# The expert down products with the weight matrix stationary and 160 rows moving, their outputs summed and turned ahead of the scatter

## The reference

```python
probs = jax.nn.softmax((hf @ router).astype(F32), axis=-1)
top_p, top_i = lax.top_k(probs, TOP_K)
top_p = top_p / jnp.sum(top_p, -1, keepdims=True)
gates = jnp.sum(jax.nn.one_hot(top_i, N_EXPERTS, dtype=F32) * top_p[..., None], axis=1)
out = jnp.zeros_like(hf)
for e in range(N_EXPERTS):          # 8 experts
    out = out + gates[:, e:e + 1] * _swiglu(hf, wg[e], wu[e], wd[e])
# _swiglu(h, wg, wu, wd) = (silu(h @ wg) * (h @ wu)) @ wd, 1024 -> 1408 -> 1024
```

## Time and profile before

| | |
|---|---|
| median of 3 runs | 3254.36 us (3253.84 to 3255.85) |
| profiled execution | 3251.81 us, span 3250.0 us |
| TensorE busy (products) | 89% of the span |
| VectorE busy | 49% |
| ScalarE busy | 33% |
| mean granted TensorE clock | 0.938 |

### The profile page before, as it was taken

The page is one execution under the profiler, slowest core; times in us unless marked ns, Lnnn a source line. Parts: engine busy times, 40 slices in busy tenths (PEclk is TensorE's granted clock), DMA queues, the critical chain, the costliest instruction groups (busy, mean ns, idle before and its releaser), DMA issues. The chain is left out here.

```text
span 3250.0 us, 41841 instructions
## 1 busy us (share of the span) xinstructions
PE 2897.2 (89%) x16468; PEld 2532.3 (78%) x16468; DVE 1606.1 (49%) x2087; ACT 1075.4 (33%) x1404; POOL 132.4 (4%) x111
## 2 busy tenths in 40 slices
PE   7999769999799997779999999969999685789997
PEld 5889768878678896679999999958788564668785
DVE  3536744232434466357777777763332437442333
ACT  2334113222232332035555555442222323242221
POOL 0012100000000220010000000000000000000000
PEclk9999989999899998879999999979999896799998
DMA  4210025151322001166767767742341210251421
GB/s 142 92 45 1 1 91 146 40 142 46 97 78 78 16 1 52 40 186 195 203 196 214 202 194 207 202 129 80 96 112 33 91 26 2 66 148 46 136 59 65
DMA packets 441223, 324.88 MB, mean 100 GB/s; under 512 B 22880, under 2 KB 395616, under 8 KB 440960
## 3 DMA queue, kind: packets, MB, share of 16 engines
q1 hardware_dynamic: 439360, 317.06, 34.1%
q0 software_dynamic: 1728, 5.90, 0.6%
HBM read 318.19 MB, written 4.72 MB: 99 GB/s over the span
## 5 line engine op out<-in xcount | busy, mean ns | idle before, releaser
L1467 PE MATMUL psum<-x_split,gate_up_split 128*128 128x512 f32 x1056 | 414.6, 393 | 15.8 <-PEq L1636 7.8
L1468 PE MATMUL psum<-x_split,gate_up_split 128*128 128x512 f32 x1056 | 413.9, 392 | 0.0
L1469 PE MATMUL psum<-x_split,gate_up_split 128*128 128x512 f32 x1056 | 413.5, 392 | 0.0
L2476 PE MATMUL psum<-x_slots_split,gate_up_split 128*128 128x320 f32 x1424 | 378.4, 343 | 4.4 <-DVE x_slots_split L2654 2.5
L1759 PE MATMUL psum<-w_split,x_split 128*128 128x256 f32 (+1 forms) x2400 | 300.0, 287 | 33.1 <-ACT w_split L1773 13.2
L1759 PEld LDWEIGHTS psum<-w_split,x_split 128*128 128x128 f32 x2400 | 295.8, 196 | 38.4 <-ACT w_split L1773 27.1
L2477 PE MATMUL psum<-x_slots_split,gate_up_split 128*128 128x160 f32 x1424 | 314.7, 241 | 0.0
L1759 PE MATMUL psum<-x_split,w_split 128*128 128x512 f32 x1248 | 295.2, 396 | 15.8 <-DVE w_split L1793 6.2
L1570 DVE TENSOR_TENSOR arena<-arena,psum 128x512 f32<-128x512 f32 x66 | 45.4, 688 | 513.9 <-ACT arena L1525 513.9
L1759 PEld LDWEIGHTS psum<-x_split,w_split 128*128 128x128 f32 x1248 | 235.5, 190 | 75.9 <-issue 20.6
L2476 PEld LDWEIGHTS psum<-x_slots_split,gate_up_split 128*128 128x128 f32 x1424 | 261.6, 189 | 10.3 <-issue 7.3
(11 more groups left out here) (423 smaller groups left out, 4485.8 us busy)
## 6 DMA issues: line engine op xcount, KB each, us to landing
arena<-in_moe_w_gate SPq DMA_DIRECT2D x91, 512.0 KB, 4.4
arena<-in_moe_w_up SPq DMA_DIRECT2D x91, 512.0 KB, 5.7
arena<-in_moe_w_down SPq DMA_DIRECT2D x176, 256.0 KB, 4.2
arena<-in_ffn_w_gu SPq DMA_DIRECT2D x88, 512.0 KB, 5.4
arena<-in_w_in SPq DMA_DIRECT2D x36, 1024.0 KB, 5.3
arena<-in_ffn_w_down SPq DMA_DIRECT2D x132, 256.0 KB, 3.3
arena<-in_ffn_w_gate SPq DMA_DIRECT2D x22, 512.0 KB, 4.1
arena<-in_ffn_w_up SPq DMA_DIRECT2D x22, 512.0 KB, 5.5
```

The costliest lines, as they stand in the source:

```text
L1467: nc.tensor.matmul(out, w[0], XR[:, 0, k, :], start=k == 0, stop=False)
L1468: nc.tensor.matmul(out, w[0], XR[:, 1, k, :], start=False, stop=False)
L1469: mm = nc.tensor.matmul(out, w[1], XR[:, 0, k, :], start=False, stop=k == DT - 1)
L2476: hi = lambda start, stop: nc.tensor.matmul(out, wt[0], XE[:, k8, :, :].rearrange("p s n -> p (s n)"), start=start, stop=stop)
```

## The change

The down products are turned round: a 128 x 128 piece of the weight matrix is stationary, and the hidden slots move (320 columns, high and low together, then 160). Four output tiles of 128 features per half lie in four banks, half 0 in banks 4 to 7 and half 1 in banks 0 to 3, with high and low sums side by side and features on partitions. VectorE adds the two sums (`turned_sums`), TensorE turns the result back (`turn_outputs`, 8 transposes per half), then the outputs are split and scattered as before. Since banks are shared anew, `turn_pick` becomes four steps in the free columns of banks 0 to 3 ahead of gate_up(1) to gate_up(4), with two small copies on ScalarE per step; `indices` goes to gate_up(8); the gather moves from ahead of down(11) to behind down(13), into banks 5 to 7; scatter(0) moves behind down(21); and the three next split_g stand in iterations 6, 7, 8 of the second half on ScalarE and VectorE, with outputs_lo(0) behind the third.

```diff
-        SBANK = (4, 5, 2, 3, 4, 5, 6, 7)
-        XB = [(k // 3, (k % 3) * N) for k in range(DT)]
+        SBANK = (6, 7, 4, 5, 6, 7, 4, 5)
+        XB = [(5 + k // 3, (k % 3) * N) for k in range(DT)]
+        YBANK = (4, 2)
@@ gate_up
                     if f >= 2:
                         wait(pe, w, halves, FU, f - 1)
+                        if 3 <= f < 7:
+                            wait(pe, w, pt_ready, TT, f - 2)
...
+                        if f == 0:
+                            wait(pe, w, yt_ready, 2, 2 * k)
...
+                    if 1 <= f <= TT:
+                        turn_pick(w, f - 1)
+                    if f == 8:
+                        indices(w, f)
@@ down
+                    for j in range(4):
+                        wt = [DSPL[:, n % FRING, s, j * P:(j + 1) * P] for s in range(2)]
+                        out = self.bank(4 - 4 * half + j, 2 * N)
+                        hi = lambda start, stop: nc.tensor.matmul(out, wt[0], HID[:, :, f, :], start=start, stop=stop)
+                        lo = lambda: nc.tensor.matmul(out[:, N:2 * N], wt[1], HID[:, 0, f, :], start=False, stop=False)
...
-                        nc.tensor.matmul(out, x[0], wt[0], start=f == 0, stop=False)
-                        nc.tensor.matmul(out, x[0], wt[1], start=False, stop=False)
-                        mm = nc.tensor.matmul(out, x[1], wt[0], start=False, stop=f == FU - 1)
...
+                def turn_outputs(w, half):
+
+                    wait(pe, w, yt_ready, 2, half + 1)
+                    if half == 0:
+                        wait(pe, w, x_lo, 3, 4)
                     for j, s0 in enumerate(TILES):
+                        for i in range(4):
+                            mm = nc.tensor.transpose(self.bank(YBANK[half] + j)[:, i * P:(i + 1) * P], YT[half][:, i, s0:s0 + P], self.cf("ident"))
+                    mm.then_inc(y_turned.sem, 1)
@@ TensorE, body
                     down(w, FU - 2)
                     down(w, FU - 1)
-                    wait(pe, w, rows_loaded, 32, 64)
-                    wait(pe, w, halves, FU, FU)
-                    gather()
                     for f in range(FU):
                         down(w, FU + f)
+                        if f == 2:
+                            wait(pe, w, rows_loaded, 32, 64)
+                            wait(pe, w, yt_ready, 2, 1)
+                            gather()
                         if f == 6:
-                            scatter(w, 0)
-
+                            turn_outputs(w, 0)
+                    scatter(w, 0)
+                    turn_outputs(w, 1)
                     gate_up(w, 0, 1)
                     scatter(w, 1)
@@ VectorE, body, second half
+                def turned_sums(w, half):
+                    wait(dve, w, d_mm, DU, (half + 1) * FU)
+                    b = 4 - 4 * half
+                    nc.vector.tensor_reduce(YT[half], self.PS[:, b * HALF:(b + 4) * HALF].rearrange("p (i c) -> p i c", i=4)[:, :, 0:2 * N]
+                                            .rearrange("p i (s n) -> p i n s", s=2), AX.X, ALU.add).then_inc(yt_ready.sem, 1)
...
-                    outputs_lo(w, 0)
+                    turned_sums(w, 0)
                     for f in range(3, FU):
-                        if f < 6:
+                        split_d(w, FU + f)
+                        if f in (3, 4, 5):
                             tokens_lo(w, f - 3, 1)
-                        split_d(w, FU + f)
-                        if f in (6, 8):
-                            split_g(w, f // 8, 1)
-                        if f >= FU - 2:
-                            add(w, e, 2 * (f - FU + 2))
-                            add(w, e, 2 * (f - FU + 2) + 1)
+                        if f in (6, 7, 8):
+                            split_g(w, f - 6, 1)
+                        if f == 8:
+                            outputs_lo(w, 0)
+                    turned_sums(w, 1)
+                    for n in range(TT):
+                        add(w, e, n)
                     outputs_lo(w, 1)
-                    split_g(w, 2, 1)
```

More of the change, by code:

```diff
@@ L1361, in close, with retire @@
                 self.spare[name] = self.counts.pop(name)
+    def retire(self, *names):
+        for name in names:
+            del self.counts[name]
     def cf(self, name):
@@ L2385, in stage_moe @@
         TILES = (0, N - P)
-        SBANK = (4, 5, 2, 3, 4, 5, 6, 7)
-        XB = [(k // 3, (k % 3) * N) for k in range(DT)]
+        SBANK = (6, 7, 4, 5, 6, 7, 4, 5)
+        XB = [(5 + k // 3, (k % 3) * N) for k in range(DT)]
+        YBANK = (4, 2)
+        AT = 2 * N
+        YT = [self.area(XR0 + 2 * D + 16 + half * 4 * N, 4, N) for half in range(2)]
+        yt_ready, y_turned = (self.sig(n) for n in ("turned_outputs_summed", "outputs_turned"))
+        pt_step = self.sig("scatter_matrix_steps")
         def before(f, L, ring=FRING):
@@ L2449, in gather, with indices @@
                     mm.then_inc(gathered.sem, 1)
-                def indices():
+                def indices(w, f):
+                    if f > 0:
+                        wait(pe, w, pick_ready, 1, 2)
                     for j, (s0, n) in enumerate(((0, P), (P, N - P))):
                         for t in range(TT):
-                            mm = nc.tensor.matmul(self.bank(6)[0:n, j:j + 1], PSEL[:, t, s0:s0 + n].bitcast(F32), self.cf("token")[:, t:t + 1],
+                            mm = nc.tensor.matmul(self.bank(2 * (f % 2))[0:n, AT + j:AT + j + 1], PSEL[:, t, s0:s0 + n].bitcast(F32), self.cf("token")[:, t:t + 1],
                                                   start=t == 0, stop=t == TT - 1)
@@ L2504, in down @@
-                    mm.then_inc(d_mm.sem, 1)
-                def turn_pick(w):
-                    wait(pe, w, acc_done, 2 * TT, 0)
+                        if f == 0:
+                            wait(pe, w, acc_done, 2 * TT, 0)
+                    elif f == 0:
+                        wait(pe, w, halves, FU, FU)
+                    for j in range(4):
[3 more added lines that the diff above has]
+                        lo = lambda: nc.tensor.matmul(out[:, N:2 * N], wt[1], HID[:, 0, f, :], start=False, stop=False)
+                        if f < FU - 1:
+                            hi(f == 0, False)
+                            mm = lo()
+                        else:
+                            lo()
+                            mm = hi(False, True)
@@ new lines, in down, with turn_pick @@
+                    mm.then_inc(d_mm.sem, 1)
+                def turn_pick(w, t):
+                    for j, s0 in enumerate(TILES):
+                        mm = nc.tensor.transpose(self.bank(2 * ((t + 1) % 2) + j)[:, AT:AT + P], PSEL[:, t, s0:s0 + P].bitcast(F32), self.cf("ident"))
+                    mm.then_inc(pick_turned.sem, 1)
+                def turn_outputs(w, half):
+                    wait(pe, w, yt_ready, 2, half + 1)
+                    if half == 0:
+                        wait(pe, w, x_lo, 3, 4)
@@ L2553, in _ @@
                 pe.wait_ge(pick_ready.sem, pick_ready.base + 1)
[L2554 removed]
+                indices(0, 0)
                 for _ in range(40):
[L2556 removed]
+                    nc.tensor.matmul(self.bank(4, P), self.cf("ident"), self.cf("ident"), start=True, stop=True)
                 pe.wait_ge(rows_loaded.sem, rows_loaded.base + 32)
@@ L2721, in _ @@
                 dve.wait_ge(idx_mm.sem, idx_mm.base + 1)
-                indices()
+                indices(0)
                 for f in range(FRING):
```

78 lines of the change are left out of this document (36 added, 42 removed).

## The result

The changed kernel takes 3302.57 us (median of four, 3298.83 to 3305.06), the kernel before in the same comparison 3255.11 (3253.84 to 3259.49): ratio 1.0142, interval 1.0125 to 1.016. It is slower by 47 us and 10.6 us above the forecast of 3292: inside the range of 3268 to 3306, and outside the forecast's own narrower range of 3284 to 3300. The profiled execution took 3300.31 us (span 3298.5); its mean granted clock is 0.928, that of before 0.938.

The account below looks back on a forecast made before the run. TensorE bounds the kernel at 5.52 us an iteration, VectorE close behind at 4.99. Lull 3.1 plus clock 1.55, times 8, is 37.5; with 3251.81 and 2.55 that gives 3292 us, range 3268 to 3306.

Parts of the forecast that it names:

- The cost of a down: TensorE's down products: 4 pairs, 1.03 us each down against 1.40 before, 0.37 saved 22 times a body.
- the bound by columns: Lower bound for a new down, counting columns alone (1920 against 3072): 0.87 us.
- the one by instructions: Upper bound for a new down, eight products at the old step of 0.233: 1.86 us.
- The first part: Body up to the gather's end: gate_up(3) still waits, to 11.13; gate_up(10) ends at 52.8, the gather at 61.76.
- G: The end of the gather in an expert body, predicted 61.76 us after the body's start, against 61.43 before.
- the rival of late token rows: Gather waits for token rows because indices are made later; a 2 us wait adds 16, 3308 us; chance 0.06.
- The lull: Behind the gather TensorE waits for down tiles VectorE has still to split, ahead of down(18) to (20); +3.1 us a body.
- VectorE's list: VectorE's in-order steps from the gather's end to the start of split_d(21): 12.9 us, against TensorE's 9.0.
- The clock: Granted clock falls behind the gaps ahead of the last downs: 3.3 us at low level, +1.55 a body (0 to 1.7).
- The lull without the clock: Rival: TensorE waits for down tiles but its clock does not fall; 3279 us, chance 0.22.
- TensorE staying the bound: Faster rival: VectorE's steps behind the gather fit into TensorE's 9 us; 6.5 a body saved, 3202 us, chance 0.11.
- The clock over the whole tail: Rival: clock stays low through two downs, two scatters and gate_up(0); 9.6 us a body, 3356 us, chance 0.06.

Follow-up runs that it names:

- run 5: run 4 with one more swap: in iteration 0 ScalarE does split_d(1) ahead of the gate tile 3 split; 3214.3 us, ratio 0.9873.
- Runs 2: Changed kernel with the split of gate tile 2 moved behind the last down tiles on both engines; 3271.77 us, ratio 1.006.
- run 4: Changed kernel with split_g(0) during the gather, split_g(1) and (2) behind the last down tile, tokens and first output split one step later; 3221.25 us.
- run 8: Changed kernel with only split_g(0) moved, behind split_d(14) into the time of the gather, on ScalarE and VectorE; 3302.42 us, ratio 1.0146.
- run 1: Changed kernel with idle TensorE products, written to an unread bank, ahead of down(18), down(19) and down(20); 3281.79 us, ratio 1.0085.
- run 6: Kernel before the change with ScalarE's split_d(1) put ahead of the gate tile 3 split in iteration 0; 3253.02 us, ratio 0.999.
- run 7: run 1 with the load of gate tile 2 also issued ahead of that of down tile 21; 3276.92 us, ratio 1.0072.
- run 9: run 8 with the load of gate tile 2 also issued ahead of that of down tile 21; 3290.84 us, ratio 1.0098.

## Why the prediction was right in sign and short in size

**The cost of a down held.** 1.03 us was predicted, 1.00 to 1.07 measured. The pairs at 320 and 160 columns do cost what gate_up's cost; neither the bound by columns (0.87) nor the one by instructions (1.86) came near. The Trainium skill, page "TensorE: Matmul & The Clock Gate", section "Back-to-back issue gap", would have let the change save next to nothing on a down; the traces have 1.40 before and 1.03 after, so the measurement decides against it here. The turn took 0.80 us (1801.06 to 1801.86, predicted 0.79), the reduce of 1280 1488 ns (predicted 1.49), and the turned pick's small copies, 260 and 361 ns, delay nothing that shows; the forecast had 0.25 for them.

**The first part held.** Predicted and measured: gate_up(3) at 11.13 and 11.20, the end of gate_up(10) at 52.8 and 52.95, G at 61.76 and 62.01. The first down's gain is lost to the wait ahead of gate_up(3), whose reason run 5 shows: with ScalarE's down tile out of VectorE's way it is gone. Down(10) waits 0.4 us for HID(10), as predicted. The gather had no wait for its rows, so the rival of late token rows did not occur.

**The lull was the cause.** Runs 2 and 4 show it: same products, same sums, only the place of the splits differs, and the time goes from 3302 to 3272 and to 3221. Down(20) was to start at G + 15.38 and started at 15.32 in this body, at 14.8 to 15.6 in the eight. The waits on VectorE were 0.73 for split_g(0) (predicted 0.98) and 0.49 for gate tile 2 (predicted 0.57; 0 to 0.79 over the eight bodies). The idle times in the profile ahead of down(18), (19) and (20) are 1.48, 1.56 and 2.34, not 1.9, 1.8 and 3.5, but these are not the same measure: the profile counts from the end of the last product's record, the prediction from when the next could have started. Counted from starts (a turn 0.79 us, a down 1.03) the rows give 1.72, 1.77 and 3.49. The forecast's own terms also hold the 0.96 ahead of down(15), which its list leaves out. One thing was not in the prediction: VectorE's list and the wait for the load stand in for each other, so that shortening the list alone (run 8) only lengthens the wait for the load.

**Terms of the sum.** The lull was put at 3.1 us a body and is about 3.45; G accounts for nearly 0.3 of that (62.03 in the mean, 61.76 predicted). The clock was put at 1.55 us and costs 2.3 (0 to 1.7 were the bounds, so this is above the upper one). The term that was mis-sized is the 3.3 us of low clock, taken from a place with one gap between dense products. Here three gaps come one after another, and behind the start of down(20), where every microsecond lies on the path, TensorE ran at the low clock for 3.4 to 6.7 us, 4.8 in the mean. The share of work lost was as assumed (a pair takes 0.48 us instead of 0.257, and 1 - 0.257 / 0.48 is 0.465, as 1 - 0.23 / 0.43): 5.5 x 0.465 = 2.5 us in the body shown, where the rows have 3.97 - 2.06 for the downs and 4.43 - 3.75 for scatter(0), 2.6. Together (0.35 + 0.75) x 8 = 9 of the missing 10.6 us; the rest is within the spread of the runs.

The start of down(20) and the time at the low clock behind it also explain why bodies with the same order of work differ. Windows of 10 us from the start of down(20), in the third, fourth and fifth body of the changed kernel (granted clock 0.83, 0.73 and 0.67, so 3.4, 5.4 and 6.6 us at the low level):

```profile
1699.08:1709.08 10.00, 10.00 (x53) 9.22 (x54) 5.21 (x7) 1.41 (x2) 0.00 (x0) 0.83 0.89 254
1792.66:1802.66 10.00, 10.00 (x46) 9.08 (x47) 4.95 (x6) 0.52 (x1) 0.00 (x0) 0.73 0.87 248
1887.04:1897.04 10.00, 10.00 (x42) 8.92 (x43) 4.89 (x6) 0.00 (x0) 0.00 (x0) 0.67 0.81 237
```

From down(20)'s start to the body's end it takes 14.62 us at full clock (run 1, 1786.08 to 1800.70). The start, plus 14.62, plus 0.465 times the time at the low level (from the record of the granted clock, which the windows view shows to two digits) gives every body's length behind G to 0.05 us:

| body | down(20) starts, G + | us at low clock behind it | sum | measured, G to end |
|---|---|---|---|---|
| 1 | 15.16 | 4.35 | 31.80 | 31.80 |
| 2 | 15.61 | 5.65 | 32.86 | 32.82 |
| 3 | 15.07 | 3.48 | 31.31 | 31.32 |
| 4 | 15.32 | 5.47 | 32.48 | 32.46 |
| 5 | 15.20 | 6.66 | 32.92 | 32.87 |
| 6 | 15.40 | 3.70 | 31.74 | 31.73 |
| 7 | 15.13 | 5.80 | 32.45 | 32.42 |
| 8 | 14.78 | 3.41 | 30.98 | 30.99 |

**The rivals.** The lull without the clock would be run 1, 3282 (3279 was forecast for it). Its condition did not occur: the clock fell in the bodies. TensorE staying the bound was refused on the right ground, VectorE's list, and was one edit of order away: run 4's 3221 and run 5's 3214 approach the 3202 of that rival. The clock over the whole tail did not occur either; it was back before scatter(0) ended in all eight bodies. That rival was also priced too low: at 0.48 us a pair instead of 0.257, two downs lose 1.8 us and gate_up(0) 3.6, not 1.1 and 2.2, so with the two scatters it would have been some 11.5 us a body and not 9.6.

**Open.** The clock fell at G + 10.6 in some bodies and as late as G + 15.2 in others, with the same order of gaps in front. What decides this was not tested; run 1 shows only that with the gaps filled it does not fall there at all.

## What to carry to other kernels

Before an engine's work is shortened, add up the list that the next engine, in order, has to do over the same stretch, not over the whole body: here VectorE was 27% idle over a body, and behind the gather had 12.9 us to do against TensorE's 9.0. A faster product needs the order of the elementwise lists laid anew: what the next stage wants last goes last, and the long steps go where the fast engine has other work. And two waits that stand in for each other are seen only when both are taken away. An edit whose gain is under the spread of the medians can still be read from the trace, from the length of a repeated body (run 6: 87.95 against 88.47 us, with medians that could not tell). Idle products hold the clock up for such a measurement, but look whether they leave the wait in place: in run 7 they ended after the tile was ready and hid part of the gain.

## What the chip showed that was not expected

- The low clock lasted longer than in the first stretch of the earlier trace rows. Down(19) ran at 1.2 GHz behind gaps of 1.48 and 1.56 us, down(20) and (21) behind 2.34 more, and the granted clock of the 10 us from 1788 is 0.50; that of the 11.8 us behind them is 0.99. The same order of work cost between 30.99 and 32.87 us from G to the body's end.
- At the low level a pair of 320 and 160 columns takes 0.48 us, 1.9 times its 0.257. The first products of both levels are 0.39 and 0.61.
- 336 idle products more (17284 against 16948 in the page's count), in gaps of TensorE, made the program 21 us faster than without them.
- An earlier issue did not land the load as much earlier. In run 9 gate tile 2's load went out at G + 0.20 and ScalarE began on it, after waiting for it, 7.9 us later at G + 8.08. In the changed kernel it went out at G + 2.93 (1780.27) and ScalarE began at G + 9.21: 2.7 us earlier on the queue gave 1.1 us. In the kernel before it took 6.4 us (1758.58 to 1765.00).
